# A two-layer hybrid decoder step on eight cores: the list scheduler's choice rule, its operation costs, the tile lag and the copy of the transposed queries

## The reference, cut to what matters

```python
for l in range(DEPTH):                       # 2 layers
    q, k, v, u = _project(hp, ln1[l], w_in[l])        # rmsnorm, 1024 -> 1280
    q, k = _rope(q, pos_p), _rope(k, pos_p)           # 16 of 64 columns
    a  = _prompt_attention(q, k, v, attn_sinks[l])    # band of 128 keys back
    pm = _pool_mix(u, pos_p, L, pool_w[l], pool_scale[l])
    hp = hp + concat(a, pm) @ w_out[l]
    hp = hp + _mlp(hp, ln2[l], w_up[l], w_down[l])    # 1024 -> 4096 -> 1024, relu squared
    ...                                      # the same for the sample tokens, with a key/value cache
y = _rmsnorm(h, ln_f)
```

## Time and profile before

| | |
|---|---|
| median of 3 runs | 3802.29 us (3802.05 to 3809.07) |
| the profiled execution's own time | 3792.41 us |
| its span on the slowest core (core 1) | 3790.9 us |
| spans of the 8 cores | 3781.6 to 3790.9 us |
| mean granted TensorE clock of the cores | 0.961 to 0.965 of full speed |
| TensorE / VectorE / ScalarE busy | 90% / 43% / 43% |
| instructions | 57785 |

### The profile page before, as it was taken

One profiled execution on the slowest core, in us unless ns is written; L12 is line 12 of the kernel. 1 busy time (PEld: TensorE's weight loads), 2 busy tenths in 40 slices (PEclk: granted clock), 3 DMA queues, 4 the chain that ended last, 5 costly groups with the idle time before them and its releaser, 6 DMA issues.

```text
span 3790.9 us, 57785 instructions; the slowest of 8 cores (3781.6 to 3790.9 us)
## 1 busy us (share of the span) xinstructions
PE 3424.8 (90%) x20571; PEld 1738.5 (46%) x20571; DVE 1615.0 (43%) x3231; ACT 1633.4 (43%) x4007; POOL 170.4 (4%) x214
## 2 busy tenths in 40 slices
PE   5899989988999899889998997899989977898798
PEld 2444444444444444344444443444444444454444
DVE  1443454344444433454344334443443443334434
ACT  2443454335434533454345333543453354334434
POOL 0000000000000000000000000000000000000000
PEclk7999999999999999899999998999999999999999
DMA  9155406550553255406522554155216532562144
GB/s 190 25 90 85 67 9 100 89 118 7 96 85 56 36 84 89 113 12 98 88 47 36 95 78 112 21 98 83 40 36 98 92 92 46 80 100 37 16 72 96
DMA packets 177394, 275.81 MB, mean 73 GB/s; under 512 B 19788, under 2 KB 103724, under 8 KB 177016
## 3 DMA queue, kind: packets, MB, share of 16 engines
q0 software_dynamic: 160544, 218.87, 37.8%
q1 hardware_dynamic: 16568, 53.23, 4.5%
HBM read 472.20 MB, written 23.13 MB: 131 GB/s over the span
## 4 chain that ended last, share of the span: by engine, by line
PE 75%; ACT 9%; DVE 9%; issue 5%; DMA 1%; DVEq 0%; ACTq 0%; another core or an unknown queue 0%; SPq 0%; POOLq 0%
PE ps_all L1001 24%; PE ps_all L982 23%; PE ps_all L605 8%; PE ps_all L934 6%; PE ps_all L1057 5%; ACT s_xhat L569 3%; DVE s_stat L741 2%; DVE s_xhat L574 2%; PE ps_all L735 2%; PE ps_all L777 1%; PE ps_all L581 1%; PE ps_all L733 1%; ACT s_P L758 1%; DVE s_h L938 1%; DMA s_win<-w_in 1%
## 5 line engine op out<-in xcount | busy, mean ns | idle before, releaser
L1006 DVE TENSOR_TENSOR s_h<-s_h,ps_all 128x512 f32<-128x512 f32 x1088 | 746.8, 687 | 1074.8 <-PE ps_all L1001 1018.1
L1001 PE MATMUL ps_all<-s_wdn,s_aT 128*128 128x512 bf16 x4352 | 1004.2, 380 | 19.5 <-ACT s_aT L992 11.4
L982 PE MATMUL ps_all<-s_xn2T,s_wup 128*128 128x384 bf16 (+1 forms) x5120 | 992.1, 347 | 3.1 <-DVE s_h L938 2.1
L987 ACT ACTIVATE s_relu<-ps_all 128x384 f32<-128x384 f32 (+1 forms) x640 | 340.6, 533 | 978.1 <-PE ps_all L982 974.5
L982 PEld LDWEIGHTS ps_all<-s_xn2T,s_wup 128*128 128x128 bf16 x5120 | 499.4, 98 | 456.4 <-issue 3.9
L1001 PEld LDWEIGHTS ps_all<-s_wdn,s_aT 128*128 128x128 bf16 x4352 | 416.5, 98 | 535.7 <-issue 79.4
L1057 PE MATMUL ps_all<-s_bmat,s_ident 128*128 128x512 bf16 x1443 | 413.0, 421 | 93.1 <-DVE s_ropet L623 13.0
L992 ACT ACTIVATE s_aT<-s_relu 128x384 bf16<-128x384 f32 (+1 forms) x640 | 359.6, 565 | 65.9 <-PE ps_all L1001 10.8
L605 PE MATMUL ps_all<-s_win,s_xnT 128*128 128x512 bf16 (+1 forms) x1632 | 308.3, 348 | 18.9 <-DMA s_win<-w_in 8.0
L758 ACT ACTIVATE s_P<-ps_all,s_stat 128x256 bf16<-128x256 f32 x528 | 243.3, 478 | 134.2 <-DVE s_stat L747 125.1
L574 DVE SCALAR_TENSOR_TENSOR s_xhat<-s_h,s_stat,s_gbc 128x1024 bf16<-128x1024 f32 x136 | 172.8, 1283 | 216.6 <-ACT s_stat L573 216.6
(11 more groups left out here) (118 smaller groups left out, 2472.4 us busy)
## 6 DMA issues: line engine op xcount, KB each, us to landing
s_wup<-w_up POOLq DMA_DIRECT2D x80, 1024.0 KB, 9.3
s_wdn<-w_dn POOLq DMA_DIRECT2D x80, 1024.0 KB, 9.5
s_win<-w_in POOLq DMA_DIRECT2D x10, 2560.0 KB, 19.3
s_wout<-w_out POOLq DMA_DIRECT2D x10, 2048.0 KB, 17.4
s_h<-x_p SPq DMA_DIRECT2D x32, 512.0 KB, 12.1
y_p<-s_h SPq DMA_DIRECT2D x32, 512.0 KB, 10.0
s_gbc<-gbc SPq DMA_DIRECT2D x20, 512.0 KB, 5.9
nks<-ck SPq DMA_DIRECT2D x2, 960.0 KB, 42.7
```

The source lines that it names most:

```text
L982: r = e.matmul(ps_t[bk][:, 0:n], lhsT=wup_t[s][:, k, fc * 128:(fc + 1) * 128], rhs=xn2T_t[:, k, t0 * 128:t0 * 128 + n], start=(k == 0), st ...
L987: act(lambda e, bk=bk, n=n, ri=ri: e.activation(out=r_t[ri][:, 0:n], in_=ps_t[bk][:, 0:n], func=AF.Relu), [ps_b[bk]], [r_b[ri]], cost=0.55)
L1001: r = e.matmul(ps_t[db + hf][:], lhsT=aT[:, fc, (t - t0) * 128:(t - t0 + 1) * 128], rhs=wdn_t[s][:, fc, hf * 512:(hf + 1) * 512], start=(f ...
L1006: dve(lambda e, t=t, hf=hf, db=db: e.tensor_tensor(out=h_t[t][:, hf * 512:(hf + 1) * 512], in0=h_t[t][:, hf * 512:(hf + 1) * 512], in1=ps_ ...
```

## The change

Four things change.

- `list_schedule` no longer takes the operation with the earliest start. It finds the earliest possible start `mn` among the engine's ready operations, and of all that can start within `CP_SLACK` = 0.3 us of it takes the one with the largest `cp`.
- Many operations get costs of their own in place of the default.
- The transposed queries (64x1024) are copied in two halves: heads 0 to 3 by ScalarE, heads 4 to 7 by VectorE (tiles other than the sample tile).
- `LAG` goes from 3 to 7. The orders of TensorE, ScalarE and VectorE that come out are the same, row for row, with 3 and with 7.

```diff
+CP_SLACK = 0.3
+ATT_LAG = 7
...
-            for idx in pend[e]:
-                st = max(tfree, ready_t[idx])
-                if PRIO_MODE == "cp":
-                    key = (st, -cp[idx], idx)
...
+            if PRIO_MODE == "cp" and CP_SLACK > 0:
+                mn = min(max(tfree, ready_t[idx]) for idx in pend[e])
+                for idx in pend[e]:
+                    st = max(tfree, ready_t[idx])
+                    if st <= mn + CP_SLACK:
+                        key = (-cp[idx], st, idx)
+                        if cand is None or key < cand:
+                            cand = key
+                cand = (cand[1], cand[0], cand[2])
...
-            act(lambda e: e.activation(out=qT[:].rearrange("p h t -> p (h t)"), in_=qTps[0:64, :], func=AF.Copy), [ps_b[bqT]], [qTb])
+            act(lambda e: e.activation(out=qT[:, 0:4, :].rearrange("p h t -> p (h t)"), in_=qTps[0:64, 0:512], func=AF.Copy), [ps_b[bqT]], [], pw=[qTb], cost=0.6)
+            dve(lambda e: e.tensor_copy(out=qT[:, 4:8, :].rearrange("p h t -> p (h t)"), in_=qTps[0:64, 512:1024]), [ps_b[bqT]], [], pw=[qTb], cost=0.35)
...
-                        [ps_b[bk]], [], pw=[Ba])
+                        [ps_b[bk]], [], pw=[Ba], cost=0.7)
...
-        LAG = 3
+        LAG = ATT_LAG
```

More of the change, by code:

```diff
@@ L151, in list_schedule @@
             cand = None
-            for idx in pend[e]:
-                st = max(tfree, ready_t[idx])
-                if PRIO_MODE == "cp":
-                    key = (st, -cp[idx], idx)
[L156 to L159, removed]
+            if PRIO_MODE == "cp" and CP_SLACK > 0:
[7 more added lines that the diff above has]
+                cand = (cand[1], cand[0], cand[2])
+            else:
+                for idx in pend[e]:
+                    st = max(tfree, ready_t[idx])
+                    if PRIO_MODE == "cp":
+                        key = (st, -cp[idx], idx)
+                    else:
+                        key = (st, idx)
+                    if cand is None or key < cand:
+                        cand = key
             k2 = (cand[0], cand[-1])
@@ L609, in att_tile @@
         qk, qkb = qk_t[par], qk_b[par]
[L610 to L613, removed]
+        act(lambda e: e.activation(out=qk[:, 0:512], in_=ps_t[bq][:, 0:512], func=AF.Copy), [ps_b[bq]], [], pw=[qkb], cost=0.7)
+        act(lambda e: e.activation(out=qk[:, 512:640], in_=ps_t[bk_][:, 0:128], func=AF.Copy), [ps_b[bk_]], [], pw=[qkb], cost=0.3)
+        act(lambda e: e.activation(out=vu_own[:, 0:384], in_=ps_t[bk_][:, 128:512], func=AF.Copy), [ps_b[bk_]], [], pw=[vu_own_b], cost=0.5)
+        act(lambda e: e.activation(out=vu_own[:, 384:640], in_=ps_t[bu][:, 0:256], func=AF.Copy), [ps_b[bu]], [], pw=[vu_own_b], cost=0.4)
         ri = info["rope"]
@@ L664, in att_tile @@
                 dve(lambda e, src=src, dst=dst: e.tensor_copy(out=dst, in_=src), [ps_b[bqT]], [qTb])
-        dve(lambda e: e.tensor_copy(out=kT_own[:].rearrange("p h t -> p (h t)"), in_=kTps[0:64, 0:256]), [ps_b[bkT]], [kT_own_b])
+        dve(lambda e: e.tensor_copy(out=kT_own[:].rearrange("p h t -> p (h t)"), in_=kTps[0:64, 0:256]), [ps_b[bkT]], [kT_own_b], cost=0.3)
         mix, mixb = mix_t[par], mix_b[par]
@@ L696, in att_tile @@
         pe(poolB, rd, [ps_b[bdT]])
-        act(lambda e: e.activation(out=dbf[:].rearrange("p g t -> p (g t)"), in_=ps_t[bdT][:], func=AF.Copy), [ps_b[bdT]], [dbfb])
+        act(lambda e: e.activation(out=dbf[:].rearrange("p g t -> p (g t)"), in_=ps_t[bdT][:], func=AF.Copy), [ps_b[bdT]], [dbfb], cost=0.7)
         yield
@@ L707, in att_tile @@
                                       in1=bcast_last(pscale_t[:, l * 4:(l + 1) * 4], 128), op=ALU.mult),
-            [ps_b[bpm], pscale_b], [], pw=[mixb])
+            [ps_b[bpm], pscale_b], [], pw=[mixb], cost=0.65)
         yield
@@ L781, in st_pt @@
                 if g == 0:
-                    act(lambda e: e.activation(out=dst, in_=ptps[:, :], func=AF.Copy), [ps_b[bpt]], [PTg[g]])
+                    act(lambda e: e.activation(out=dst, in_=ptps[:, :], func=AF.Copy), [ps_b[bpt]], [PTg[g]], cost=1.0)
                 else:
-                    dve(lambda e: e.tensor_copy(out=dst, in_=ptps[:, :]), [ps_b[bpt]], [PTg[g]])
+                    dve(lambda e: e.tensor_copy(out=dst, in_=ptps[:, :]), [ps_b[bpt]], [PTg[g]], cost=0.6)
             def st_pv(g):
```

16 lines of the change are left out of this document (8 added, 8 removed).

## The result

The changed kernel takes 3876.8 us (median of 10 runs), the kernel before, on the same chip, 3806.7. Some executions of every kernel run longer, with a lower granted clock on one die, and the ratios leave them out. The ratio is **1.019, 95% interval 1.0174 to 1.0207**: 72 us slower (66 to 79). The forecast was slower by 11. The profiled execution shows the same: its span is 3865.3 us, 74.4 more than before.

What follows compares the result with a forecast made beforehand. Attention-stage pairs were taken to be bound by a chain: projection, scores, maxima, exponentials, output projections, norms. Terms 37 + 6 - 16 - 12 - 6 + 2 = +11 us gave 3803, or 3813 on the median's footing; range 3758 to 3846.

Steps and rivals of the forecast that it cites:

- first rival: Regular pairs: ScalarE's train of exponentials doesn't set the end, so the 4.5 us are slack; sum -38, 3764 us, chance 0.25.
- It cancels: Whole kernel, a rival: lead and overlap, with terms of both signs, even out within 0.2%; 3802 us, chance 0.15.
- second rival: Fillers overrun and hold up TensorE: +31, sum +42, 3844 us, chance 0.15; sign: batches of 5 and 6 over 2 us.
- Term 1: The 12 regular pairs: 4.5 us of lead lost, 1.4 of gaps won back, 3.1 a pair, +37 us (-24 to +60).
- behind the train ... as before: Regular pairs, after the last exponentials: sink's part, division and transposes unchanged, with smaller filler batches replacing the one of 4.
- Term 5: Parts counted at nothing: last pairs of stages with 7 tiles zero, program start +2, lag zero, DMA orders hardly moved.
- Its order is the same there: Middle of an MLP stage: TensorE's order is the same in both programs, so nothing to be had or lost.
- The queues' orders hardly move: DMA queues: orders nearly unchanged, nothing moved in the pair; a late weight load would show only at a stage's first projection.
- term 3: First layer of groups 3 and 4: three tiles half a tile apart take 87 us, not 95.0; -16 (-24 to 0).
- The last pairs: Last pair of the eight stages with 7 tiles: later scores, but train cut by the first projection; zero (-8 to +12).
- Term 2: First tiles going alone in five stages: reductions before the first maximum, and changed filler batches; +6 us (0 to +15).
- term 4: Last group: four pairs go side by side, -12 (-20 to 0); the sample tile's rounds, -6 (-12 to +3).

Runs made afterwards that it cites:

- e8: Changed kernel with 8 us more scheduler priority for the two small operations that make each negated maximum; ratio 1.0045 to the kernel before, +17 us.
- e11: Changed kernel, orders kept, 752 fillers in place of 1646; no ratio, profiled cores 4 to 7 take 3862 to 3875 us against 3857 to 3864.
- e4: Changed kernel with each group's first-tile load put directly behind the store freeing its slot in SyncE's queue; no ratio, profiled span 3870.8 us against 3865.3.

## Why the prediction was right or wrong

**Right: direction and mechanism.** Six reductions ahead of the first negated maximum, the first exponential at +11.4 us (computed: 11.4), a lead of 4.5 lost, no gap behind it. "It is slack" (first rival) is refuted by e8: with 2.6 of the 4.5 given back, 55 us come back. "It cancels" did not happen. The second rival's sign did show: of the batches in the chain, the one of 6 takes 2.72 us, over the 2 that I had named.

```profile
1314.19 2.72 PE L1070 MATMUL ps_all<-s_bmat,s_ident 128*128 128x512 bf16 x6 [1.01 <-ACT s_P L771]
```

But it lies within ScalarE's train, which has no gap from 1313.03 to its end at 1322.43, and by e11 fewer fillers give no faster kernel. So the sign was badly chosen, and fillers were not what the change lost.

**Term 1, too small: 3.1 a pair forecast, 4.8 measured.** The train itself came out near what I worked out: the last exponential ends 2.7 us later. The step that failed is "behind the train ... as before". Before, the first tile's output projection ran 2.3 us behind the train; now it starts 3.6 behind:

```profile
1324.80 0.60 PE L824 MATMUL ps_all<-s_ident,s_a 128*128 128x128 bf16 x4
```

Here TensorE transposes both halves of the first tile's attention at once, behind the last products of both tiles (1323.92) and 2 more fillers. ScalarE's two copies of them follow, until 1325.87, and only then comes the output projection. Before, both copies were done at 1278.59, and the projection stood directly behind the last products. With 2.7 for the train and 1.3 for this, 4.0 of the pair's 4.2 us are told. The pair also stood for 12: the others lost 3.4 to 6.9, and why they differ stays open.

**Term 5, the larger miss: +50 where I counted +2.** Three steps failed. "Its order is the same there" was read in the middle of an MLP stage and carried to its first rows, where transposes and fillers now stand first: 2 us each. "The queues' orders hardly move" was wrong in three entries, and these moved the first load; but by e4 they cost little net (nothing on core 1), since **term 3**'s -16, measured as -18.6, is their other side: stretch and three tiles together gave 1 us. The honest sum for term 3 was near zero. The start (+7) lost by the same late maxima, which I had priced only in the pairs: e8 gives 6 of it back. The last pairs (+8) did not come back in e8 (3 us longer still), so what lengthens them stays open.

**Term 2** was +6, measured 0; **term 4** was -18, measured -13.

**On the clock** I gave additional fillers nothing, against the Trainium skill (TensorE: Matmul & The Clock Gate, Part 1), by which activity releases the throttle. e11 agrees: with half the fillers the granted clock of an attention stage falls from 0.92 to 0.85. But the change's 203 extra ones raised nothing that can be seen: the cores' mean clock is 0.961 to 0.965 before, 0.962 to 0.968 after, and between the first and last exponential of eight pairs it is 0.88 before and 0.72 after (core 1).

The whole answer in one line: truer costs for VectorE, put into a rule that takes the longest remaining chain among nearly equal starts, queue reductions ahead of the two small operations for which ScalarE waits.

## What to carry to other kernels

In a list scheduler, a truer cost can make a worse order: what counts is which operations become candidates at the same time. After each edit look at the first operation for which the next engine waits, and count what is queued ahead of it. Test rule and costs apart and together: here one is -35, the other +21, both +93. And when two stages meet, add the stretch between them to the stage before calling either a gain.

The version to keep is the rule with the old costs and the whole copy: 0.9909 of the time before.

## What the runs showed that I had not expected

Taking away half of the useless matmuls did not make the kernel faster. The projection shows where the time went, before the comma busy us, behind it mean ns of a matmul; core 4, first the change, then e11:

```profile
L617 PE MATMUL ps_all<-s_win,s_xnT 128*128 128x512 bf16 x1088 | 305.4, 387 | 22.1 <-DMA s_win<-w_in 12.2 <-DVE s_xnT L598 5.2 <-DVE s_ropet L634 3.3
```

```profile
L617 PE MATMUL ps_all<-s_win,s_xnT 128*128 128x512 bf16 x1088 | 341.3, 420 | 30.7 <-DMA s_win<-w_in 12.7 <-DVE s_xnT L598 10.5 <-DVE s_ropet L634 5.0
```

So a stage that waits for ScalarE pays for the fillers it lacks in its next projection: 36 us over the kernel.
